# Head norms of the first mixer: eight-column roots between the two blocks of scores, spread by transposes

## What is computed

```python
o_hg = hgrn2_chunkwise(q, log_f, k, v)                    # 4 heads x 128
o_hg = rms_norm(o_hg, hg_out_norm[i]).reshape(B, S, HG_WIDTH) * jax.nn.silu(hg)
...
o_mla = causal_block_attention(qf, kf, v)                 # 4 heads x 128, keys of 128 + 64
h = h + jnp.concatenate([o_hg, o_mla], axis=-1) @ w_out[i]
```

## Time and profile before

| | us |
|---|---|
| Median of three runs | 1484.86 |
| Lowest and highest | 1483.26, 1485.17 |
| The profiled execution | 1485.67 |
| Its span, first to last instruction | 1483.90 |
| TensorE busy | 1351.0 (91%) |
| VectorE busy | 943.2 (64%) |
| ACT busy | 554.5 (37%) |
| GpSimd busy | 557.5 (38%) |

### The profile page before, as it was taken

One profiled execution on the slowest core, in us unless ns is written; L12 is line 12 of the kernel. 1 busy time (PEld: TensorE's weight loads), 2 busy tenths in 40 slices (PEclk: granted clock), 3 DMA queues, 4 the chain that ended last, 5 costly groups with the idle time before them and its releaser, 6 DMA issues.

```text
span 1483.9 us, 20938 instructions
## 1 busy us (share of the span) xinstructions
PE 1351.0 (91%) x7726; PEld 1032.1 (70%) x7726; DVE 943.2 (64%) x1827; ACT 554.5 (37%) x1003; POOL 557.5 (38%) x379
## 2 busy tenths in 40 slices
PE   9999999999999999999999999987887788778877
PEld 8999999978999999899999866433333333333332
DVE  3777454445577645485553775887777767777755
ACT  4444355425444445555654322321122222222312
POOL 3444446411344545000302344544453444444440
PEclk9999999999999999999999999999899998998999
DMA  6777663212577654255336699999999999999996
GB/s 251 263 278 281 251 233 140 98 57 95 205 273 276 244 192 150 86 199 183 130 115 255 281 421 417 420 422 422 422 423 422 422 421 422 422 422 421 422 422 260
DMA packets 60055, 428.00 MB, mean 288 GB/s; under 512 B 6673, under 2 KB 6993, under 8 KB 8913
## 3 DMA queue, kind: packets, MB, share of 16 engines
q0 software_dynamic: 36864, 268.45, 43.5%
q1 hardware_dynamic: 22320, 156.90, 29.4%
q10 hardware_dynamic: 800, 1.70, 0.3%
HBM read 425.98 MB, written 1.05 MB: 288 GB/s over the span
## 4 chain that ended last, share of the span: by engine, by line
PE 64%; DMA 23%; DVE 7%; issue 3%; ACT 2%; POOL 0%; DVEq 0%; POOLq 0%; ACTq 0%; SPq 0%
DMA rows_w<-in_expert_uv,arena 17%; PE ps L530 11%; PE ps L525 11%; PE ps L526 11%; PE ps L1050 6%; PE ps L1054 5%; DMA rows_x<-in_expert_uv,arena 4%; PE ps L1006 3%; PE ps L613 2%; PE ps L611 2%; PE ps L612 2%; DMA arena<-in_expert_uv,arena 2%; PE ps L564 1%; PE ps L555 1%; PE ps L709 1%
## 5 line engine op out<-in xcount | busy, mean ns | idle before, releaser
L390 POOL TENSOR_TENSOR wlo<-ring,whi 128x1024 fp32r<-128x1024 f32 x98 | 249.5, 2548 | 403.1 <-ACT whi L1149 403.0
L1149 ACT ACTIVATE whi<-ring 128x1024 fp32r<-128x1024 f32 x220 | 230.1, 1057 | 307.7 <-PE ps L530 150.6
L525 PE MATMUL ps<-nh,whi 128*128 128x256 f32 x1312 | 329.3, 288 | 5.3 <-ACT nh L1167 2.8
L526 PE MATMUL ps<-nh,wlo 128*128 128x256 f32 x1312 | 323.3, 283 | 0.0
L390 DVE TENSOR_TENSOR wlo<-ring,whi 128x1024 fp32r<-128x1024 f32 x122 | 171.3, 1415 | 169.1 <-ACT whi L1149 168.3
L525 PEld LDWEIGHTS ps<-nh,whi 128*128 128x128 f32 x1312 | 251.7, 192 | 10.4 <-issue 3.7
L526 PEld LDWEIGHTS ps<-nh,wlo 128*128 128x128 f32 x1312 | 251.8, 192 | 0.1
L530 PE MATMUL ps<-nl,whi 128*128 128x256 f32 x1312 | 191.1, 286 | 0.1
L530 PEld LDWEIGHTS ps<-nl,whi 128*128 128x128 f32 x1312 | 171.5, 192 | 4.8 <-DVE nl L1578 1.2
L2266 POOL DMA_INDIRECT arena<-in_expert_uv,arena x91 | 101.3, 1113 | 158.0 <-PE ps L1054 118.4
L2063 DVE CUSTOM_DVE_ANT_0 arena<-arena 128x1024 f32<-128x1024 f32 x91 | 110.9, 1223 | 48.8 <-DMA arena<-in_expert_uv,arena 47.9
(11 more groups left out here) (365 smaller groups left out, 2421.8 us busy)
## 6 DMA issues: line engine op xcount, KB each, us to landing
ring<-in_w SPq DMA_DIRECT2D x112, 1024.0 KB, 4.8
arena<-in_wmod SPq DMA_DIRECT2D x24, 1024.0 KB, 4.8
arena<-in_w SPq DMA_DIRECT2D x6, 1024.0 KB, 9.0
small<-in_small SPq DMA_DIRECT2D x2, 938.5 KB, 8.2
arena<-in_expert_uv,arena POOLq DMA_INDIRECT x91, 25.6
rows_w<-in_expert_uv,arena POOLq DMA_INDIRECT x68, 24.5
h<-in_x SPq DMA_DIRECT2D x2, 512.0 KB, 5.1
keys<-in_keys SPq DMA_DIRECT2D x1, 1024.0 KB, 6.9
```

Of the source, the lines that this page charges most:

```text
L390: return v.tensor_tensor(wlo[:, tile % TILES, :], ring[:, tile // 2 % RAW, at:at + TILE], whi[:, tile % TILES, :].bitcast(F32), ALU.subtract)
L525: mm(to, hi[:, k, :], nh[:, k, :], start=(k == 0), stop=False)
L526: mm(to, lo[:, k, :], nh[:, k, :], start=False, stop=False)
L1149: fn(whi[:, tile % TILES, :], ring[:, slot % RAW, at:at + TILE], ACT.Copy).then_inc(S("high_w"), 1)
```

## The change

The sums of squares get one column for each head and block of 128 tokens instead of a whole row of copies: the squares are the weights and a single column of ones is the moving operand, so that a column of bank 4 holds the sums of 128 tokens, one token to a partition. `attention` takes a function `between`, called between its two blocks of scores, and `hg_sums` is put there. ACT takes the root of eight columns and right after it runs an exponential of a constant, into a place that nothing reads. VectorE inverts the eight columns ahead of the logits. Behind the scores TensorE spreads them with eight transposes of a broadcast column into banks 2 and 3, and VectorE's scaling reads the inverses from there.

```diff
-        csq, osq, ostd = sq[:, 0:3, :], sq[:, 0:HH, :], sq[:, HH:C, :]
+        csq, osq = sq[:, 0:3, :], sq[:, 0:HH, :]
+        hg_root, hg_inverse = sq[:, HH, 0:TB * HH], sq[:, HH, TB * HH:2 * TB * HH]
...
-            def attention(n, score):
+            def attention(n, score, between=None):
...
                     score(hd, 0, ps[:, 5, hd * P:(hd + 1) * P])
+                if between:
+                    between()
                 for hd in range(4):
...
                 pe.wait_ge(S("hg_squared"), 1)
-                for j in range(2):
-                    last = mm(ps[:, 2 + j, :], ones[:, :], osq[:, 2 * j:2 * j + 2, :], start=True, stop=True)
+                for hd in range(HH):
+                    for b in range(TB):
+                        i = TB * hd + b
+                        last = mm(ps[:, 4, i:i + 1], osq[:, hd, b * P:(b + 1) * P], ones[:, 0:1], start=True, stop=True)
                 last.then_inc(S("hg_sums"), 1)
+
+            def hg_spread():
+
+                pe.wait_ge(S("ple_copied"), 2)
+                pe.wait_ge(S("hg_inverted"), 1)
+                for hd in range(HH):
+                    for b in range(TB):
+                        i, at = TB * hd + b, hd % 2 * T + b * P
+                        last = nc.tensor.transpose(ps[:, 2 + hd // 2, at:at + P],
+                                                   hg_inverse[:, i:i + 1].to_broadcast([P, P]), ident)
+                last.then_inc(S("hg_spread"), 1)
...
             pe.wait_ge(S("rope_done"), 1)
-            attention(0, mla_score)
-            pe.wait_ge(S("ple_copied"), 2)
-            hg_sums()
+            attention(0, mla_score, hg_sums)
+            hg_spread()
             pe.wait_ge(S("hg_copied"), 1)
...
             act.wait_ge(S("hg_sums"), 1)
-            fn(ostd[:, :, :].rearrange("p h t -> p (h t)"), ps[:, 2:4, :].rearrange("p b n -> p (b n)"), ACT.Sqrt,
-               bias=eps[:, 0:1], scale=1.0 / P).then_inc(S("hg_std"), 1)
+            fn(hg_root, ps[:, 4, 0:TB * HH], ACT.Sqrt, bias=eps[:, 0:1], scale=1.0 / P).then_inc(S("hg_std"), 1)
+            fn(std[:, 0, 0:1], eps[:, 0:1], ACT.Exp)
...
+            dve.wait_ge(S("hg_std"), 1)
+            v.reciprocal(hg_inverse, hg_root).then_inc(S("hg_inverted"), 1)
             logits(0, m, float(QK) ** -0.5)
 
-            dve.wait_ge(S("hg_std"), 1)
-            own(v.reciprocal(osq[:, 0:2, :], ostd[:, 0:2, :]))
             inverses(0, m)
-            own(v.reciprocal(osq[:, 2:HH, :], ostd[:, 2:HH, :]))
             dve.wait_ge(S("hg_copied"), 1)
+            dve.wait_ge(S("hg_spread"), 1)
             for hd in range(HH):
-                ins = v.scalar_tensor_tensor(ho[:, hd, :], ho[:, hd, :], V("hg_norm", hd), osq[:, hd, :], ALU.mult, ALU.mult)
+                ins = v.scalar_tensor_tensor(ho[:, hd, :], ho[:, hd, :], V("hg_norm", hd),
+                                             ps[:, 2 + hd // 2, hd % 2 * T:(hd % 2 + 1) * T], ALU.mult, ALU.mult)
             own(ins)
```

## The result

The changed kernel's median is 1493.47 us (1490.32 to 1495.86, five runs) against 1483.92 us for the kernel before (1483.26 to 1485.17, five runs). The ratio is 1.0061, with a 95% interval of 1.0044 to 1.0078: slower, where the forecast was 1485.3 us with a range up to 1487.6. The profiled execution of after is one of the faster ones, 1491.39 us with a span of 1489.6 us.

What follows compares the result with a forecast made beforehand. TensorE's queue was taken to bind: 1.62 (sums) + 0.88 (transposes) - 1.82 (old sums) = +0.68, less 0.24 us of wait, +0.44; 1484.86 + 0.44 = 1485.3 us, range 1482.6 to 1487.6.

Steps and rivals of the forecast that it cites:

- The mechanism: Rival: TensorE's clock falls to half at the one-column sums, from the scores on; 3.3 us lost, 1488.6 us, chance 0.09.
- the only row there was: Profile row with the clock at 0.50 near two-column norm sums; 6.6 us at half pace, priced at 3.3 us.
- TensorE has no idle at all until 342: Argument against the falling clock: behind the new one-column burst TensorE's queue has no idle until 342 us.
- the burst at 592.02: Later norm's two-column sums, eight records in 0.81 us at clock 1.00; used to price the new sums and against a fall.
- the fill: 24 keep_busy records on TensorE ahead of the turned probabilities, 336.10 to 338.77, 2.67 us; expected unchanged.
- The row of 607: Clock at 0.50 from about 607.7 to 614.6, in a later norm's two-column sums while TensorE has nothing to do.
- the sums of one column: Eight products, 16 records, between the blocks of scores: 1.62 us of TensorE's queue, at most 1.8.
- The eight transposes: Spread of the inverses behind the scores: eight records, 0.88 us on TensorE, at most 1.76.
- The queue's balance: TensorE up to the second half of the turned probabilities: +0.68 us of work less 0.24 us of wait, +0.44 us.
- the 2.4 us won on ACT and VectorE: Second inverses ready at 337.5, 2.4 us earlier, hidden by TensorE's queue; rival that it comes through: 1482.5 us, chance 0.08.
- nothing waits for the roots: Inverses of the eight columns stand at 328.8, so the transposes at 332.4 don't wait; cover 3.7 us.
- a missing early table load: Rival: table load still ahead of the exponentials; inverses at 338.8, ahead of 340.3, time as forecast; chance within the forecast's 0.76.

Runs made afterwards that it cites:

- e2: The changed kernel with the one-column sums behind both blocks of scores and the transposes behind the embedding products; 1487.00 us (1.0028).
- e1: The changed kernel with 128 columns of ones for each sum instead of one, in banks 2 and 3; 1485.85 us (1.0014).
- e6: The changed kernel with 128-column sums, and without the twelve fill products ahead of the turned probabilities; 1480.26 us (0.9983).
- e12: The kernel before without the twelve fill products ahead of the turned probabilities; 1485.68 us (1.0008).
- e10: The changed kernel with 128-column sums, without the twelve fill products and without the exponential of a constant; 1481.98 us (0.9981).
- e3: The changed kernel with the inverses spread by ordinary products, two records each, instead of transposes; 1494.02 us (1.0061).
- e8: The kernel before with its 512-column sums moved between the blocks, early root and exponential table, reciprocals reordered on VectorE, fill cut to two products; 1483.81 us (1.0001).
- e11: The changed kernel with six fill products, 12 records, directly behind the one-column sums; 1491.17 us (1.0034).
- e4: The kernel before with eight unused one-column products, 16 records, added between the two blocks of scores; 1490.08 us (1.0039).
- e9: The changed kernel with 32 columns of ones for each sum instead of one; 1491.26 us (1.0047).

## Why the prediction was wrong

The step that failed is the clock: the sum put it at nothing, and the granted clock fell to 0.50 for 13.6 us. The mechanism was among the rivals, at 0.09 and a price of 3.3 us; it is what happens, and it costs about twice that, 6.3 us in the profiled execution, as the fall lasts 13.6 us and not 6.6. The price was taken from the only row there was, and its length didn't carry over: in the five traces with a fall behind such a burst it is 6.8, 10.2, 10.2, 13.6 and 17.1 us.

The argument against it was made in two sentences, and both leaned on the wrong thing. "TensorE has no idle at all until 342" is true, and no protection: the clock went down while TensorE was busy throughout. And the burst at 592.02 is eight two-column records between dense products of 256 columns, while ours is sixteen records behind scores that take 0.42 us for two records of 128 columns, where the fill takes 0.22 for two (24 records in 2.67 us). So ours does not stand "between dense work". Half the length in denser company is not the nearest row for the clock, though it was the nearest one for the duration. The row of 607 was read as little work and idleness together, and the rival was discounted because idleness was missing; that little work might do without any was not weighed.

By the prediction's own steps: the sums of one column took 1.81 us where nothing disturbed them (e2: 328.34 to 330.15), not 1.62; the upper bound given, 1.8, was the better figure, 0.113 us a record. That the weight load sets this pace fits the 1.81 us that 16 records take with 1 and with 32 columns, and 1.88 with 128. The eight transposes are eight records and take 0.93 us in e1, 0.88 foretold. The queue's balance is 20.8 us to the second half in e1 against 20.1 before, +0.7, and +0.6 at the last copy, where +0.44 was the sum; most of the 0.2 is the sums (1.88 us in e1). That TensorE's queue binds and that the 2.4 us won on ACT and VectorE stay without effect held: e1 shows it with the clock up, e6 and e12 show which fill hid it. That nothing waits for the roots held: the inverses stand 8.7 us after the first recurrent product, 9.0 were allowed. That a missing early table load would cost nothing held too, though for a better reason than the slack: the load is not late at all (e10).

With e1 beside it, most of the slowdown is one thing: 7.6 us for the columns. What is left, 1485.85 against 1483.70, has an interval of 0.6 to 3.4 us, and the mixer's trace gives +0.6, its lower end. The part beyond 0.6 us was not traced to a place, nor was the difference between 7.6 and the 6.3 us of the traces; a longer fall in the slower runs, as in e3, would give it, but no trace of them was kept.

## What to carry to other kernels

Where every product brings a weight load of its own, don't thin out its columns to save time: here 128 columns cost 0.07 us more than one over 16 records, and in this place 1 or 32 columns lost the clock and 128 kept it. A stretch that shows 100% busy can still lose its clock, so read the granted clock of the stretch, not only its gaps. And when a wait is shortened, cut the fill that was put in to cover it, or nothing is gained; then read the clock again, as e8 and e12 lost it for some microseconds where fill was gone.

## What the runs showed of the hardware that was not expected

The clock fell with no gap in TensorE's records. Behind the first block of scores stood 16 records of one column (or of 32), back to back. The fall came 0.6 us (e3), 0.7 (e11) and 1.6 (after) behind the burst's first record, and 3.1 in e4 and e9, where the burst was over. The clock then stayed at half for 17.1, 6.8, 13.6, 10.2 and 10.2 us of uninterrupted work. What sets the moment and the length is not shown. The Trainium skill (TensorE: Matmul & The Clock Gate, Why this matters for your kernels) puts drops of the clock in mid-kernel down to idle gaps between bursts; here there was none, and the measurement decides. The rule of the Trainium skill that transposes count less (TensorE: Matmul & The Clock Gate, Part 4: PE-mode transpose), set against the change in the prediction, finds no support here: the clock was already down when they came, eight transposes between scores and products leave it at 1.00 in e1, and ordinary products in their place (e3) did not bring it back sooner.

A switch of ACT's tables cost the load and no more: the root ends at 326.05, the load runs from 326.06 to 327.34, and the next function starts at 327.36. The Trainium skill (ScalarE: Activation LUTs, What ACT_TABLE_LOAD costs) adds a drain of about 1.38 us to each switch of sets; the trace has 1.31 us for the whole of it.
